# A 4-layer encoder step in fp32r halves: 128 unused bytes in place of 64 between weights and activations in SBUF

## What is computed

```python
for i in range(DEPTH):                      # mixers: stick-breaking, conv, GLA, stick-breaking
    o = mix[i % 3](rms_norm(h, norm_mix[i]))   # w_in: 1024x3072, w_out: 1024x1024
    h = h + o
    h = h + sq_relu_mlp(rms_norm(h, norm_mlp[i]), mlp_w_up[i], mlp_w_down[i])  # 1024x4096x1024
y = rms_norm(h, norm_final)
```

## The kernel before, in words

| tensor | bytes | start, past a multiple of 128 |
|---|---|---|
| X, big | 18432, 55296 | 0 |
| raw (w_f is another name for whi and wlo) | 16384 | 64 |
| whi, wlo | 16384 each | 64 |
| apart | 64 | 64 |
| ahi, alo (also mixs) | 18432 each | 0 |
| hhi, hlo (also stg; the first 4096 bytes also rankw) | 18432 each | 0 |

## Time and profile before

### The profile page before, as it was taken

One profiled execution on the slowest core, in us unless ns is written; L12 is line 12 of the kernel. 1 busy time (PEld: TensorE's weight loads), 2 busy tenths in 40 slices (PEclk: granted clock), 3 DMA queues, 4 the chain that ended last, 5 costly groups with the idle time before them and its releaser, 6 DMA issues.

```text
span 2762.2 us, 48400 instructions
## 1 busy us (share of the span) xinstructions
PE 2731.4 (99%) x20754; PEld 2659.4 (96%) x20754; DVE 1266.0 (46%) x1577; ACT 857.4 (31%) x933; POOL 223.2 (8%) x232
## 2 busy tenths in 40 slices
PE   8999999999999999999999999999999999999998
PEld 8986999999999999999999899999999969999998
DVE  4258534333455434334478543333342494433433
ACT  3147322122312323223224432222331384221222
POOL 4000100000211100000233110000010001000001
PEclk9999999999999999999999999999999999999999
DMA  4211322222222222222212122222222103322221
GB/s 147 88 66 32 111 92 77 92 78 90 77 92 76 77 92 77 91 77 79 90 47 76 40 89 80 89 79 90 78 94 90 47 36 120 98 76 92 76 91 50
DMA packets 205540, 223.64 MB, mean 81 GB/s; under 512 B 3766, under 2 KB 200480, under 8 KB 205392
## 3 DMA queue, kind: packets, MB, share of 16 engines
q1 hardware_dynamic: 200992, 206.06, 23.3%
q0 software_dynamic: 4400, 15.41, 1.6%
HBM read 208.60 MB, written 12.86 MB: 80 GB/s over the span
## 4 chain that ended last, share of the span: by engine, by line
PE 96%; DVE 1%; ACT 1%; issue 0%; DMA 0%; POOL 0%; SPq 0%; ACTq 0%; DVEq 0%
PE bank L395 88%; PE bank L500 2%; PE bank L460 1%; PE bank L521 1%; PE bank L692 1%; PE bank L468 0%; PE bank L560 0%; PE bank L640 0%; PE bank L415 0%; PE bank L747 0%; DMA big<-in_x_prompt 0%; DVE wlo L1183 0%; PE bank L454 0%; DVE e L1288 0%; PE bank L746 0%
## 5 line engine op out<-in xcount | busy, mean ns | idle before, releaser
L395 PE MATMUL bank<-ahi,whi 128*128 128x288 f32 x3584 | 770.0, 295 | 8.2 <-DVE alo L1208 6.8
L395 PE MATMUL bank<-alo,whi 128*128 128x288 f32 x3584 | 766.0, 295 | 0.0
L395 PE MATMUL bank<-ahi,wlo 128*128 128x288 f32 x3584 | 762.8, 294 | 0.0
L852 ACT ACTIVATE whi<-raw 128x2048 fp32r<-128x2048 f32 x191 | 364.4, 1908 | 832.2 <-PE bank L395 825.5
L395 PEld LDWEIGHTS bank<-ahi,whi 128*128 128x128 f32 x3584 | 573.3, 188 | 13.1 <-DVE wlo L1183 7.0
L395 PEld LDWEIGHTS bank<-ahi,wlo 128*128 128x128 f32 x3584 | 575.5, 188 | 0.0
L395 PEld LDWEIGHTS bank<-alo,whi 128*128 128x128 f32 x3584 | 575.5, 188 | 0.0
L395 PE MATMUL bank<-hhi,whi 128*128 128x288 f32 x2560 | 549.0, 295 | 3.8 <-DVE hlo L1544 2.0
L395 PE MATMUL bank<-hlo,whi 128*128 128x288 f32 x2560 | 547.7, 295 | 0.0
L395 PE MATMUL bank<-hhi,wlo 128*128 128x288 f32 x2560 | 545.4, 294 | 0.0
L1183 DVE TENSOR_TENSOR wlo<-raw,whi 128x2048 fp32r<-128x2048 f32 x192 | 444.1, 2313 | 208.7 <-ACT whi L852 206.1
(11 more groups left out here) (247 smaller groups left out, 1514.6 us busy)
## 6 DMA issues: line engine op xcount, KB each, us to landing
raw<-in_mlp_w_up SPq DMA_DIRECT2D x64, 1024.0 KB, 5.4
raw<-in_mlp_w_down SPq DMA_DIRECT2D x64, 1024.0 KB, 5.1
raw<-in_sb_w_qkv SPq DMA_DIRECT2D x24, 1024.0 KB, 5.2
raw<-in_conv_w_in SPq DMA_DIRECT2D x12, 1024.0 KB, 5.2
raw<-in_gla_w_in SPq DMA_DIRECT2D x12, 1024.0 KB, 5.3
raw<-in_sb_w_o SPq DMA_DIRECT2D x8, 1024.0 KB, 5.2
out<-mixs POOLq DMA_DIRECT2D x2, 2048.0 KB, 7.6
out<-big POOLq DMA_DIRECT2D x2, 2048.0 KB, 8.2
```

What stands on the lines that cost most here:

```text
L395: mm = pe.matmul(acc[h][:, 0:HALF], w[:, u, k, m * P:(m + 1) * P], a[:, k, h * HALF:(h + 1) * HALF], start=(k == 0 and w is whi and a is a ...
L852: act.activation(whi[:, 1 - u], raw[:, 1 - u], ACT.Copy).then_inc(w_hi, 1)
```

## The change

The unused tensor doubles. Everything declared after it starts 64 bytes later, and nothing else changes: no instruction is added, removed or moved.

```diff
-        apart = sb("apart", [P, 16], F32)
+        apart = sb("apart", [P, 32], F32)
         mixs = passing("mixs", [P, 9216], F32)
         ahi = sb("ahi", [P, KC, T], F32R)
         alo = sb("alo", [P, KC, T], F32R)
```

## The result

The median went from 2761.3 us to 2780.8 us (four executions of each, the three of before that were shown and one more). The ratio is 1.0071, with a 95% interval of 1.0059 to 1.0083: slower by 0.7%, some 19.5 us. That is the first slower rival, priced at 2783 us, and not the forecast of 2760. Two executions in all, one of before (3319.8 us, mean granted clock 0.75) and one at a difference of 112 (5152.2 us, 0.90), were far longer than the rest and enter no ratio.

A forecast was written before the change was run, and what follows sets the result against it. TensorE's 18432 L395 matmuls at 132.23 ns were taken to bound the kernel: 2437 + 325 + 0 = 2762 us of span, as before. The forecast for the median was 2760.2 us, range 2738 to 2797.

The forecast's parts named there:

- the first slower rival: L395: reads in the same phase collide, at L669's steady distance, 1.27 ns per matmul, +23 us, 2783 us; chance 0.27.
- What bounds the kernel: TensorE in L395: 18432 matmuls at 132.23 ns make 2437 us, with 325 us for everything else.
- The 64s bit: L395 operand starts differ by 64 beyond a multiple of 128 before, by a plain multiple after; nothing else leaves a trace.
- I take zero from it: L669, already at the new relation, was taken to show no effect for L395; bounds +1.3 and -2.2 ns per matmul.
- the -2.2: Lower bound in ns per matmul for L395, from L669's first eight at 130 against 132.23.
- no change: L395's distance doesn't depend on the 64s bit: 2755 to 2766 us, chance 0.58.
- The +37 us: Upper price of the slower rival in L395: an 8 ns slip once in four matmuls atop 132.23 ns, 2797 us.
- The weighing of the skill: Two separate TensorE read ports mean no placing returns the 9.7 ns; the gap formula's 122.5 ns fits L415, not L395.
- the 9.7 ns: Part of each L395 matmul's 132.2 ns beyond the stream's 122.5, from stream and weight load together; 179 us over 18432.
- The rest of the kernel at nothing: Other TensorE work, VectorE and ScalarE, mostly inside the 325 us or under TensorE: 0.0 us, bounds -0.6 and +0.6.
- The faster rivals: L395's present phase has the collision: -22 or -41 us, chance 0.12; or all 9.7 ns goes: -179 us, 0.03.
- the smaller one: L395's present collision ends: -1.2 ns per matmul, 2738 us, or at 130 ns 2719 us; chance 0.12.

The follow-up runs named there:

- slices: Activations written as slices of one tensor, against the kernel before, to set other start differences; control at 64: 2760.9 us, ratio 1.0001.

## Why the prediction was wrong

**What bounds the kernel.** Right, and the whole difference lies there: 18432 matmuls, 132.23 before and 133.33 after.

**The 64s bit as the only thing that changes.** Right: the kernels with one operand moved are slow, with both moved fast.

**The step that failed** is the price taken for it: "I take zero from it". The row for that bit was L669, and it had been read right in its steady part: 133.5 ns, or +1.3, where L395 came out at 133.33, or +1.10. L669's own pattern, one slip in four matmuls, is what L395 falls into at the new difference. It was set aside for two reasons. One was that it "can't be the address alone", since the first eight matmuls don't show the slip at the same relation. That was wrong: the first slip comes as the tenth distance before, as the twelfth after and as the fourth without the unused tensor, all at the same relation, so early matmuls of a stretch are no evidence. The other was that L669's order of operands differs from L395's. That was wrong at this difference: L670 (that is L669, one line down), with `rankw` 64 past `ahi`, has L395's 132.2 in spite of its own order, and the exchange of the two inner loops at 64 changes nothing. That the slip lay in the `ahi` pair only followed from where it set in: after, the first pair of 0.28 us is one with `alo`.

The 130 ns that the prediction read for the first eight of L669 was rounding: to the nanosecond they are 131.25 ns apart, which is the -1 that it called as likely, and not the -2.2 that it took for its bound.

**The slower rival.** Right in place and in what it hangs on, two starts on the same residue of 128, and nearly in price: +23 us priced, +19.5 measured. Its chance was 0.27, below that of no change. The +37 us, a slip on top of the present distance, was too much. The slip's size was right, 8 ns priced and 9 measured (140 against 131), but between slips the matmuls are nearer than before, 131 and not 132.2, so that 133.33 is the mean of both. That it is a collision of two reads is still an inference. Shown is that for starts at 0 and 64 both operands' addresses enter only through their difference, which no cause on one side alone can give.

**The weighing of the skill.** The Trainium skill, "SBUF — State Buffer", section "Who interferes with whom", gives TensorE two independent read ports. The prediction drew from it that no placing would matter, and the measurement differs from that: 409.60 against 406.20 us for the same 3072 matmuls by a shift of 64 bytes of either operand, and 416.41 at a difference of 72. Whether the two ports meet somewhere, no run shows. For the other, the gap formula of "TensorE: Matmul & The Clock Gate", section "Back-to-back issue gap", which the page gives for an isolated matmul: its 122.5 ns for 288 columns isn't reached at any of the eleven differences tried, the nearest being 131.68 in a long stretch and 130.0 in 48 matmuls. So most of the 9.7 ns does not hang on the starts modulo 128 that were tried, and what makes it is open.

**The rest of the kernel at nothing.** Right: L521, L964 and L1294 have the same means as before, and the loads of transposes from `big` and `stg` take 140 ns for 141.

**The faster rivals.** No gain at 0 modulo 128 in the mean. But 130 ns, the lower price of the smaller one, does occur there, in three pieces of 48 matmuls, and a gain of 0.55 ns is real at 112, when a stretch settles so.

Open: why 72 is worst, what decides how a stretch settles at 0, 48 and 112, what the unit and the true period are (0 and 128 unused bytes agree, and 32 and 160; no pair was tried with slices), and whether it is the difference alone off multiples of 64, since the weights were moved only by 64.

## What to carry to other kernels

Where fp32r matmuls run back to back and each brings its own weight load, treat the difference of the two operands' starts modulo 128 as a parameter, measure a few values, and pin it by a named spacer: here it is worth 0.7%, and any edit of a tensor declared between them can lose it. When the whole effect of a change hangs on one property, look for the one place in the trace of before that already has the other value, and let its steady part weigh more than reasons why it might be special. Here 32 matmuls of 18432 were enough. Before a pattern of a few nanoseconds is called uneven, ask whether the rounding of the view makes it so.

## What the runs showed of the hardware

The mean distance between dense 288-column fp32r matmuls is 133.33 ns to 0.01 at six differences out of eleven, 132.23 at 64, 132.86 at 16 and 135.55 at 72 (weights 64 past a multiple of 128). At 0 it is made of three distances of 131 ns and one of 140; at 32 of 135 and 132 in turn. At 112 it took 131.68 or 133.33, from one execution and one stretch to the next, with the same instructions and addresses, and 132.23 with the loops exchanged. That is a source of spread between executions (2751.7 to 2769.7 us) at a granted clock of 1.00 and 84 GB/s in stretches at either distance. The kernel without the unused tensor spreads too, from 2769.7 to 2780.0 us, and there only the longest execution was traced. At 0 three pieces of 48 matmuls ran at 130.0 ns in one execution of the kernel after.
